# Index scores on VectorE: one running sum per head, or broadcast multiplies and a tree of adds, with ScalarE and VectorE call order changed around them

## What is computed

```python
def dsa_attention(q, k, v, iq, ik, iw):
    n_top = min(DSA_TOPK_MAX, S // 4)
    def chunk(i):
        ...
        logits = jnp.einsum('bhcd,bsd->bhcs', iqc, ik).astype(jnp.float32) * (IDX_DIM ** -0.5)
        score = jnp.einsum('bch,bhcs->bcs', iwc.astype(jnp.float32), jax.nn.relu(logits))
        score = jnp.where(kpos[None, :] <= qpos[:, None], score, -jnp.inf)
        _, sel = lax.top_k(score, n_top)
        ...
```

## Time and profile before

| | |
|---|---|
| median of 3 runs | 1250.51 us |
| lowest and highest | 1250.21 and 1251.45 us |
| the profiled execution | 1251.52 us, of which its span 1249.8 us |
| PE busy | 1228.5 us (98%), 6398 matmuls |
| DVE busy | 814.7 us (65%) |
| ACT busy | 664.4 us (53%) |
| POOL busy | 196.5 us (16%) |
| mean granted clock of TensorE | 0.997 |

### The profile page before, as it was taken

One profiled execution on the slowest core, in us unless ns is written; L12 is line 12 of the kernel. 1 busy time (PEld: TensorE's weight loads), 2 busy tenths in 40 slices (PEclk: granted clock), 3 DMA queues, 4 the chain that ended last, 5 costly groups with the idle time before them and its releaser, 6 DMA issues.

```text
span 1249.8 us, 16857 instructions
## 1 busy us (share of the span) xinstructions
PE 1228.5 (98%) x6398; PEld 1037.9 (83%) x6398; DVE 814.7 (65%) x979; ACT 664.4 (53%) x983; POOL 196.5 (16%) x174
## 2 busy tenths in 40 slices
PE   8999999999999999999999999999999999999998
PEld 6778888888887888888888899888997788888886
DVE  5899655545669966545447756876685697655544
ACT  5667454444555765443436355655547745644443
POOL 5885100001178730000000000000000030000000
PEclk9999999999999999999999999999999999999999
DMA  7523454556362254655545464343334455555551
GB/s 267 189 87 141 149 218 174 200 182 216 124 228 99 100 186 142 228 185 184 199 172 186 169 236 170 137 152 122 114 120 165 172 185 186 201 200 177 192 210 43
DMA packets 32795, 212.73 MB, mean 170 GB/s; under 512 B 3777, under 2 KB 3905, under 8 KB 10082
## 3 DMA queue, kind: packets, MB, share of 16 engines
q1 hardware_dynamic: 32674, 211.82, 47.5%
q0 software_dynamic: 64, 0.13, 0.0%
HBM read 210.88 MB, written 1.05 MB: 170 GB/s over the span
## 4 chain that ended last, share of the span: by engine, by line
PE 85%; DVE 6%; ACT 4%; POOL 2%; DMA 2%; issue 1%; SPq 0%; DVEq 0%; ACTq 0%; POOLq 0%
PE bank L599 25%; PE bank L601 25%; PE bank L600 25%; PE bank L1048 2%; DVE wlo L1765 2%; ACT probs L1367 2%; ACT whi L1290 1%; PE bank L883 1%; PE bank L629 1%; PE bank L794 1%; DMA raw<-in_w_out 1%; DVE z L2250 1%; PE bank L754 1%; PE bank L728 1%; POOL gain L518 1%
## 5 line engine op out<-in xcount | busy, mean ns | idle before, releaser
L1765 DVE TENSOR_TENSOR wlo<-raw,whi 128x2048 fp32r<-128x2048 f32 (+4 forms) x197 | 445.0, 2263 | 241.5 <-ACT whi L1290 239.5
L1290 ACT ACTIVATE whi<-raw 128x2048 fp32r<-128x2048 f32 (+5 forms) x201 | 369.3, 1842 | 131.5 <-PE bank L601 123.2
L599 PE MATMUL bank<-whi,hT_hi 128*128 128x512 f32 (+4 forms) x1028 | 401.6, 391 | 1.1 <-DVE wlo L1765 1.0
L601 PE MATMUL bank<-whi,hT_lo 128*128 128x512 f32 (+4 forms) x1028 | 392.5, 382 | 0.0
L600 PE MATMUL bank<-wlo,hT_hi 128*128 128x512 f32 (+4 forms) x1028 | 392.2, 382 | 0.0
L599 PEld LDWEIGHTS bank<-whi,hT_hi 128*128 128x128 f32 x1028 | 193.8, 189 | 38.6 <-issue 2.7
L601 PEld LDWEIGHTS bank<-whi,hT_lo 128*128 128x128 f32 x1028 | 193.4, 188 | 35.8
L600 PEld LDWEIGHTS bank<-wlo,hT_hi 128*128 128x128 f32 x1028 | 194.0, 189 | 32.6
L599 PE MATMUL bank<-whi,mixT_hi 128*128 128x512 f32 (+1 forms) x248 | 95.4, 384 | 0.2 <-DVE wlo L1765 0.2
L599 PE MATMUL bank<-whi,ffT_hi 128*128 128x512 f32 x240 | 93.7, 390 | 0.0
L601 PE MATMUL bank<-whi,ffT_lo 128*128 128x512 f32 x240 | 93.5, 390 | 0.0
(11 more groups left out here) (288 smaller groups left out, 1453.0 us busy)
## 6 DMA issues: line engine op xcount, KB each, us to landing
raw<-in_ff_loop SPq DMA_DIRECT2D x90, 1024.0 KB, 4.8
raw<-in_w_groups SPq DMA_DIRECT2D x64, 1024.0 KB, 4.7
raw<-in_w_out SPq DMA_DIRECT2D x8, 1024.0 KB, 5.6
raw<-in_ff_first SPq DMA_DIRECT2D x6, 1024.0 KB, 4.8
raw<-in_w_values SPq DMA_DIRECT2D x8, 728.0 KB, 4.1
raw<-in_w_comp SPq DMA_DIRECT2D x4, 1024.0 KB, 6.4
raw<-in_ff_last SPq DMA_DIRECT2D x3, 1024.0 KB, 4.7
raw<-in_w_values SPq DMA_DIRECT2D x4, 736.0 KB, 5.4
```

The costliest lines, as they stand in the source:

```text
L599: eng.matmul(out, lhsT=hi, rhs=wh, start=start, stop=False)
L601: return eng.matmul(out, lhsT=lo, rhs=wh, start=False, stop=stop)
L1290: eng.activation(whi[j][:, 0:n], raw[j][:, 0:n], ACT.Copy).then_inc(hi_ready, 1)
L1765: eng.tensor_tensor(wlo[j][:, 0:n], raw[j][:, 0:n], whi[j][:, 0:n].bitcast(F32), ALU.subtract).then_inc(lo_ready, 1)
```

## The change

Each relu gets a place of its own: u = 0 and 1 in `probs[:, 0]` and `probs[:, 1]`, u = 2 to 5 in four quarters of `mix`, so ACT's wait for `idx_acc` goes, and the semaphore with it. `index_sum` now does a whole half of the rows at once: it multiplies each place in one instruction by its head weights, spread over the keys by a broadcast, and then adds the heads as a tree. For the first half of the rows these are 2 multiplies on 512 elements and adds on 512, 256 and 128; for the second half 4 multiplies on 512 and adds on 1024, 512 and 256: 12 instructions a layer. The calls on ACT and DVE around it stand in another order. PE's, POOL's and SP's lists are as before.

```diff
+        def index_part(u):
+            if u < 2:
+                return probs[:, u, :]
+            return mix[:, (u - 2) // 2, (u % 2) * COLS:(u % 2 + 1) * COLS]
...
             def index_relu(l, u):
                 eng.wait_ge(idx_ready, l * 6 + u + 1)
-                if u >= 3:
-                    eng.wait_ge(idx_acc, l * 6 + u - 2)
-                eng.activation(probs[:, u % 3, :], bank[2 + u % 3][:, :], ACT.Relu, scale=(HD * IDX_HEADS) ** -0.5)\
+                eng.activation(index_part(u), bank[2 + u % 3][:, :], ACT.Relu, scale=(HD * IDX_HEADS) ** -0.5)\
                    .then_inc(idx_relu, 1)
...
-                heads_copy(l, 1, 0); scale_heads(l, 0); index_relu(l, 0); hi(4, 0); index_relu(l, 1); hi(4, 1)
-                index_relu(l, 2); copy_z(l, 3, 0); index_relu(l, 3); square_heads(l, 1, 0); copy_z(l, 3, 1)
-                index_relu(l, 4); heads_copy(l, 2, 0); square_heads(l, 1, 1); index_relu(l, 5)
-                scale_heads(l, 1); hi(5, 0); heads_copy(l, 2, 1); hi(5, 1); copy_z(l, 4, 0)
+                heads_copy(l, 1, 0); scale_heads(l, 0); index_relu(l, 0); index_relu(l, 1); hi(4, 0)
+                hi(4, 1); copy_z(l, 3, 0); index_relu(l, 2); index_relu(l, 3); square_heads(l, 1, 0)
+                copy_z(l, 3, 1); index_relu(l, 4); heads_copy(l, 2, 0); index_relu(l, 5)
+                heads_copy(l, 2, 1); square_heads(l, 1, 1); hi(5, 0); scale_heads(l, 1); hi(5, 1)
+                copy_z(l, 4, 0)
...
-            def index_sum(l, u):
-                eng.wait_ge(idx_relu, l * 6 + u + 1)
-                r, keys = (0, P) if u < 2 else (1, SEQ)
-                acc = index[:, 0:P] if u < 2 else index[:, P:3 * P]
-                for i, h in enumerate(index_heads(u)):
-                    part, w = probs[:, u % 3, i * keys:(i + 1) * keys], z[:, r, IW + h:IW + h + 1]
-                    if h == 0:
-                        ins = eng.tensor_scalar(acc, part, w, None, ALU.mult)
-                    else:
-                        ins = eng.scalar_tensor_tensor(out=acc, in0=part, scalar=w, in1=acc, op0=ALU.mult,
-                                                       op1=ALU.add)
...
+            def index_sum(l, r):
+                for u in (range(2, 6) if r else range(2)):
+                    eng.wait_ge(idx_relu, l * 6 + u + 1)
+                    n, first = (2 if r else 4), IW + index_heads(u)[0]
+                    part = index_part(u).rearrange("p (n k) -> p n k", n=n)
+                    w = z[:, r, first:first + 2 * n - 1:2].unsqueeze(2).to_broadcast([P, n, COLS // n])
+                    dve(eng.tensor_tensor(part, part, w, ALU.mult))
+                dve.wait(eng)
+                if r:
+                    half, quarter, out = mix[:, 0, :], mix[:, 0, 0:COLS], index[:, P:3 * P]
+                    dve(eng.tensor_tensor(half, half, mix[:, 1, :], ALU.add))
+                    dve.wait(eng)
+                    dve(eng.tensor_tensor(quarter, quarter, mix[:, 0, COLS:D], ALU.add))
+                else:
+                    quarter, out = probs[:, 0, :], index[:, 0:P]
+                    dve(eng.tensor_tensor(quarter, quarter, probs[:, 1, :], ALU.add))
+                    dve.wait(eng)
+                    dve(eng.tensor_tensor(quarter[:, 0:SEQ], quarter[:, 0:SEQ], quarter[:, SEQ:2 * SEQ], ALU.add))
+                dve.wait(eng)
+                n = SEQ if r else P
+                dve(eng.tensor_tensor(out, quarter[:, 0:n], quarter[:, n:2 * n], ALU.add))
+                dve.wait(eng)
...
-                head_sums(l, 0, 0); lo(3, 1); head_sums(l, 0, 1); index_sum(l, 0); lo(4, 0); index_sum(l, 1)
-                lo(4, 1); head_sums(l, 1, 0); index_sum(l, 2); index_sum(l, 3); head_sums(l, 1, 1)
-                index_sum(l, 4); index_sum(l, 5); topk_rounds(0, 2); lo(5, 0); attend_mask(A + 0, causal, (0,))
-                head_sums(l, 2, 0); lo(5, 1); attend_mask(A + 0, causal, (1,)); head_sums(l, 2, 1)
+                head_sums(l, 0, 0); lo(3, 1); head_sums(l, 0, 1); lo(4, 0); lo(4, 1); head_sums(l, 1, 0)
+                index_sum(l, 0); head_sums(l, 1, 1); lo(5, 0); lo(5, 1); attend_mask(A + 0, causal, (0,))
+                index_sum(l, 1); head_sums(l, 2, 0); attend_mask(A + 0, causal, (1,)); head_sums(l, 2, 1)
+                topk_rounds(0, 2)
                 topk_rounds(2, 3); attend_mask(A + 0, causal, (2,)); topk_rounds(3, 5); attend_copy(A + 0)
```

More of the change, by code:

```diff
@@ L218, in block_one_and_two @@
         idx_relu = sem("idx_relu")
-        idx_acc = sem("idx_acc")
         scores = sem("scores")
@@ L1844, in head_sums @@
                                   ALU.add).then_inc(ssq_ready, 1)
-            def index_sum(l, u):
-                eng.wait_ge(idx_relu, l * 6 + u + 1)
-                r, keys = (0, P) if u < 2 else (1, SEQ)
-                acc = index[:, 0:P] if u < 2 else index[:, P:3 * P]
-                for i, h in enumerate(index_heads(u)):
-                    part, w = probs[:, u % 3, i * keys:(i + 1) * keys], z[:, r, IW + h:IW + h + 1]
-                    if h == 0:
-                        ins = eng.tensor_scalar(acc, part, w, None, ALU.mult)
-                    else:
-                        ins = eng.scalar_tensor_tensor(out=acc, in0=part, scalar=w, in1=acc, op0=ALU.mult,
-                                                       op1=ALU.add)
-                    if i == (3 if u < 2 else 1):
-                        ins.then_inc(idx_acc, 1)
-                        eng.wait_ge(idx_acc, l * 6 + u + 1)
-                    else:
-                        dve(ins)
-                        dve.wait(eng)
+            def index_sum(l, r):
[20 more added lines that the diff above has]
+                dve.wait(eng)
             def topk_rounds(a, b):
```

## The result

| | before | after |
|---|---|---|
| median | 1250.45 us (1250.21 to 1251.45, 4 runs) | 1266.03 us (1265.79 to 1266.97, 4 runs) |
| ratio | | 1.0124, 95% interval 1.0112 to 1.0136 |
| span of the profiled execution | 1249.8 us | 1264.1 us |
| mean granted clock | 0.997 | 0.992 |

The change costs 15.6 us. The forecast was +9.0 (1259.5 us, range 1252 to 1265): the direction and the place were right, the size was not, and the time lies just outside the range. It is the 1266 that the prediction had worked out as its far end, with every cost at its highest.

What follows compares the result with a forecast made beforehand. PE, busy 98% of the span, was taken as the bound. Each layer wins 3.9 us at the first stall but ends 4.5 late: 2 x 4.5 = +9.0 on 1250.5 gives 1259.5 us, range 1252 to 1265.

Steps and rivals of the forecast that it cites:

- far end: Upper case: `lo(5, 1)` at 3.3 us, index sum 9.4, clock price 3; 7.7 us lost a layer, 1266 us.
- The first stall: PE's wait ahead of the MoBA scores goes, with its slow clock: 2.3 + 1.6 = 3.9 us gained a layer.
- The next wait: PE stands at the last eight transposes of `group_turn(0)` for tile 2's exponentials, 80.8 to 88.3, over 7 us.
- index sum: DVE's second-half sum: 4.9 us undisturbed, 7.8 at mean loss, 9.4 with POOL between all instructions; 8.4 taken.
- full alternation: POOL gets a turn between all seven instructions of the second-half sum on DVE, which then takes 9.4 us.
- `lo(5, 1)`: DVE's low part after ACT's split ending at 66.55: 2.54 us, range 2.2 to 3.3, ending at 69.1.
- DVE's fixed list: DVE's masks, head sums, causal add and three top-k rounds from `lo(5, 1)` through tile 2's mask, without gap: 9.65 us.
- The clock: PE falls to the lower clock behind the second stall too: at least 1.6 us, up to 3.
- Downstream: To the attention part's end, POOL waits absorb a little of PE's 5.2 us; DVE's 4.1 stays; 4.5 a layer taken.
- (c): Rival: second stall costs more clock and POOL's chain of layer 1 moves fully; 1263 to 1266 us, 12%.
- idles early, for the splits: DVE now idles early, waiting for splits, and has index-sum and top-k work behind the mask of tile 0.
- The rule weighed in the prediction: Skill's advice to minimize chained VectorE instructions: 16 becoming 12 would make DVE 0.8 us earlier, against 2.8 us more streaming.

Runs made afterwards that it cites:

- e5: Kernel after with 38 matmuls on 512 columns, result unread, ahead of the last eight transposes of `group_turn(0)` to keep PE busy; 1264.91 us, ratio 1.0120.
- e3: Kernel after with the masks of tiles 1 and 2 and both `head_sums` of set 2 ahead of the second index sum on DVE; 1267.14 us, ratio 1.0126.
- e7: Kernel after with one DVE call moved: the first half's index sum ahead of `lo(4, 0)`; 1267.28 us, ratio 1.0136.
- e10: Kernel after, DVE reordered: index sums ahead of `lo(4, 0)` and `lo(5, 0)`, masks of tiles 1 and 2 before top-k, rounds 4 and 5 behind `lo(6, 0)`; 1254.26 us.
- e1: Kernel after (tree sums, own places) with DVE's and ACT's calls in nearly the order of the kernel before; 1265.03 us, ratio 1.0113.
- e11: Kernel before with `heads_copy(l, 2, 1)` earlier on ACT, masks of tiles 1, 2 before top-k, rounds 4, 5 behind `lo(6, 0)`, `head_sums(l, 2, 1)` behind the first round; 1255.71 us.
- e4: Kernel after with POOL only scaling the two differential head sets, their rotation left out (output differs); 1255.81 us, ratio 1.0040.
- e2: Kernel after with heads added one by one as before (16 instructions, 3072 elements) in place of the trees; 1261.67 us, ratio 1.0086.
- e12: e10 with the head-by-head sums of e2 in place of the trees; 1250.53 us, ratio 1.0001.

## Why the prediction was right in direction and too small

**The first stall goes: right.** The scores start without a wait in both layers.

**The next wait: right in place, too short by 1.9 us. This is the step that failed.** It was to be 7.5 us (80.8 to 88.3) at the last eight transposes; it is 9.36. On before's clock the mask of tile 2 ends at 89.4 and not at 87.15, 2.2 later. Two terms of the sum carry that. The **index sum** was taken at 8.4 with an end at 9.4, and lasted 9.83 (70.03 to 79.86), beyond the end, in layer 1 the same: the alternation with POOL is complete. All four multiplies take 1.4 us each in the mean, undisturbed 0.6, and even the instruction on 1024 loses 0.4 (1.65 against 1.23). The prediction drew 8.4 between a mean loss of 0.41 for an instruction and full alternation; the mean came from a stretch in which POOL was idle for 2.26 us. The **`lo(5, 1)`** was taken at 2.54, ending at 69.1; it took 3.01 and ended at 69.9, part of it from a PE that came 0.27 later behind a small new wait for POOL. Together they are 2.2 us a layer, 4.4 of the 6.6 that the forecast was short. The 9.65 us of DVE's fixed list measured 9.62 (68.72 to 70.03, and 79.86 to 88.17).

**The clock: too small on PE, and nearly without weight.** 1.6 was the price of a 2.3 us stall, with up to 3 allowed; behind 9.4 us it is 1.8 in layer 0 and 2.8 in layer 1. e5 shows it to be worth nothing in layer 0 and about 1.1 in layer 1.

**Downstream: absorption that didn't come.** PE was to come out 5.2 late and DVE 4.1, and waits for POOL to take some of PE's 5.2, down to 4.5. Measured for layer 0, PE is 7.6 late at the next scores, `lo(6, 0)` 6.75, and the layer 7.2. DVE's 4.1 and the 2.2 of the two terms make 6.3, so DVE's lateness reaches the end of the layer whole, and a little comes on top; e5, with PE earlier and the layer no shorter, says that in layer 0 it is DVE that carries it. The 4.5 plus 2.2 are 6.7 of the 7.2; the other 0.5 is a remainder: the waits for POOL took up less than the 0.7 of the forecast. Layer 1 costs 8.1, and the clock of e5 covers the difference. The two layers make 15.3 us against 9.0: 4.4 from the two DVE terms, some 1 from the absorption, some 1 from the clock.

The rival that comes nearest is (c), 1263 to 1266 us, at 12%, and the time is at its end. It got there for another reason: (c) put the excess on clock and POOL's chain, and most of it was DVE's time ahead of the mask.

**The reason for a loss at all** was put on the mask of tile 2 first, and on DVE's lateness at `lo(6, 0)` behind it. e3 shows that the mask can go and the loss stays: PE waits 9.6 us at the next place. What the runs show is the order in which DVE is tied to others. `lo(5, 0)` and `lo(5, 1)` can't start before ACT's high parts, and the one of `lo(5, 1)` waits for PE to free the ring buffer (1.53 us of ACT's wait, up to 63.84). The change put the second sum behind them, into the stretch in which PE waits for all that DVE does, and left DVE idle ahead of them: 6.6 us in three waits (4.60, 0.60, 1.41) against 2.31 before. e7 shows that moving the first sum into this idle time wins nothing, since the end of it is fixed from outside; e10 shows that another order of DVE's calls, with the second sum ahead of both low parts, gives back 11.8 us. How much of that is the place of the sum and how much the top-k rounds put behind `lo(6, 0)` is not shown. The prediction did say that DVE "idles early, for the splits", but took it as a remark and gave it no price.

**The rule weighed in the prediction** (fewer chained instructions) would have had DVE 0.8 us earlier. The trees cost 3.7 to 13.8 us in three orders with four instructions fewer. The 2.8 us of streaming that the prediction set against it show in full only where POOL leaves the head-by-head sum room: in e10's order DVE spends 13.4 us a layer on the two sums as trees (4.1 and 9.3) and 10.4 head by head (5.1 and 5.3), in the order of after 15.6 either way.

What stays open: why the trees cost 13.8 us in the order of before against 4 in the others. In e1 two top-k rounds stand between the second sum and `lo(5, 0)`, which starts at 76.19 (in e10 at 67.87), and the first sum stands behind `lo(4, 0)`, ahead of which DVE idles 4.11 us; how much each of the two gives was not measured apart. Nor was it tried to move POOL's rotations instead of DVE's sums.

## What to carry to other kernels

Before work is moved on an engine with a fixed list, mark in the list the instructions whose start is set from outside (here the low parts, by a ring buffer that PE frees). In this case work behind such a mark was paid by everyone who waits for that engine, wherever the first wait then showed (e3), while idle time ahead of it could be filled only by work whose inputs were ready there (e7, e10). Take nothing for "absorbed downstream" unless the engine that is late has idle time there. And when calls are reordered, follow each of them to its readers on other engines: in e11 one small `head_sums` behind a top-k round held ACT for 4.7 us. When two engines slow each other in a stretch, take the full alternation for the forecast (here even that was 0.4 us short), and a mean from another stretch only if the other engine was as busy there.

## What the runs showed of the hardware

VectorE instructions with two SBUF inputs and POOL's slow each other: beside POOL's rotations a VectorE multiply on 512 elements takes 1.4 us in the mean instead of 0.62 in e4, and the whole tree 9.8 instead of 5.0, in other orders 10.3, 9.3 and 9.3 us (e1, e3, e10). In such a stretch the number of instructions counts beside the streamed elements: eight instructions on 256 take 8.9 us (e2), seven with 3840 elements in all 9.8. What an instruction costs depends on what the other engine has to do: the same eight take 5.3 us where POOL is idle for 2.9 of the 5.3 us (e12).

A stall of PE costs more than its length on PE itself, 1.8 and 2.8 us behind waits of 9.36 us with the mean granted clock at 0.54 in the window from 82 to 92, and yet no more than about 1.1 us of the kernel's time, as another engine was late as well (e5).
